# Two transformer blocks on one core: the halves of the values around the first pair, gate columns stationary, weighted sums one pair later, another order of the output units, x ahead of the weights

## The reference

```python
def first_block(x, ...):
    x = x + 0.5 * swiglu(rmsnorm(x, ff1_norm), w_gate, w_up, w_down)       # 2816 hidden columns
    h = rmsnorm(x, mix_norm)
    a_in, q, k, v, g_logits = split(h @ w_in)
    y_a = gmlp_spatial_gating(gelu(a_in), ...)
    y_b = stick_breaking_attention(q, k, v)     # 16 heads of 64, "stick"
    g_a, g_b = split(sigmoid(g_logits + b_gate))
    x = x + (g_a * (y_a @ w_branch_a) + g_b * (y_b @ w_branch_b)) @ w_out
    x = x + 0.5 * swiglu(rmsnorm(x, ff2_norm), ...)
    return rmsnorm(x, final_norm)

def second_block(x, ...):
    # layer 0: "moba"; with one block of 256 keys a causal softmax with a distance penalty
    # layer 1: "fox"; k, v and the gate from rms_norm(h, kv_norm):
    #   c = cumsum(log_sigmoid(hn @ w_f + b_f)); logit[t, s] += c[t] - c[s]
    for layer in range(2):
        h = h + merge_heads(mix) @ w_o[layer]
        h = h + squared_relu_mlp(rms_norm(h, mlp_norm[layer]), w_up[layer], w_down[layer])   # 4096 hidden
    return rms_norm(h, final_norm)
```

## Time and profile before

| | |
|---|---|
| runs, median (lowest to highest) | 1277.91 us (1277.82 to 1281.05) |
| the profiled execution, its time | 1278.92 us |
| its span, first to last instruction | 1277.2 us |
| mean granted TensorE clock | 0.992 |
| busy: TensorE, its weight loads | 97%, 83% |
| busy: VectorE, ScalarE, GpSimd | 64%, 50%, 14% |
| DMA | 213.20 MB on SP's queue, 173 GB/s over the span |

### The profile page before, as it was taken

One profiled execution on the slowest core, in us unless ns is written; L12 is line 12 of the kernel. 1 busy time (PEld: TensorE's weight loads), 2 busy tenths in 40 slices (PEclk: granted clock), 3 DMA queues, 4 the chain that ended last, 5 costly groups with the idle time before them and its releaser, 6 DMA issues.

```text
span 1277.2 us, 17745 instructions
## 1 busy us (share of the span) xinstructions
PE 1237.6 (97%) x6854; PEld 1055.8 (83%) x6854; DVE 823.2 (64%) x1272; ACT 636.6 (50%) x1012; POOL 176.3 (14%) x231
## 2 busy tenths in 40 slices
PE   6999999999999999999999999999999899999997
PEld 5788887898878878888878878888888887888886
DVE  4666667454686666666675757866654676786754
ACT  5444446555644346444456656544435465653442
POOL 0222220122030003221202310000000650000000
PEclk9999999999999999999999999999998999999999
DMA  6666655434646454565653445766551555575550
GB/s 193 204 217 213 209 189 175 124 111 140 219 146 228 144 166 153 191 199 198 198 181 117 140 149 182 259 201 190 190 166 34 166 170 169 173 251 194 186 178 34
DMA packets 175389, 221.77 MB, mean 174 GB/s; under 512 B 9804, under 2 KB 104632, under 8 KB 175304
## 3 DMA queue, kind: packets, MB, share of 16 engines
q1 hardware_dynamic: 173112, 213.20, 52.3%
q0 software_dynamic: 1888, 6.38, 1.6%
...
q10 hardware_dynamic: 304, 1.05, 0.2%
HBM read 219.53 MB, written 1.06 MB: 173 GB/s over the span
## 4 chain that ended last, share of the span: by engine, by line
PE 76%; DVE 10%; DMA 5%; ACT 3%; POOL 3%; issue 1%; SPq 1%; ACTq 0%; DVEq 0%; POOLq 0%
PE bank L1301 48%; PE bank L1381 15%; PE bank L1388 8%; DVE w_lo L882 5%; DMA raw<-in_ff_w_up 4%; POOL work L521 3%; ACT w_hi L584 1%; DVE work L935 1%; PE bank L1512 1%; PE bank L1324 1%; DVE xt L917 1%; PE bank L1499 1%; SPq L282 1%; DVE work L949 1%; ACT xt L621 1%
## 5 line engine op out<-in xcount | busy, mean ns | idle before, releaser
L882 DVE TENSOR_TENSOR w_lo<-raw,w_hi 128x512 fp32r<-128x512 f32 (+1 forms) x496 | 511.3, 1050 | 245.7 <-ACT w_hi L584 244.0
L584 ACT ACTIVATE w_hi<-raw 128x512 fp32r<-128x512 f32 (+1 forms) x496 | 431.9, 897 | 288.4 <-DMA raw<-in_ff_w_up 94.5
L1381 PE MATMUL bank<-xt,w_hi 128*128 128x512 f32 x1216 | 321.1, 396 | 4.1 <-DVE work L935 2.3
L1381 PEld LDWEIGHTS bank<-xt,w_hi 128*128 128x128 f32 x1216 | 216.5, 190 | 43.0 <-DVE work L935 3.2
L1388 PEld LDWEIGHTS bank<-xt,w_lo 128*128 128x128 f32 x1216 | 170.8, 190 | 15.4
L1388 PE MATMUL bank<-xt,w_lo 128*128 128x256 f32 x1216 | 175.2, 282 | 0.0
L1301 PE MATMUL bank<-w_hi,xt 128*128 128x512 f32 x512 | 161.6, 397 | 1.9 <-DVE w_lo L882 1.1
L1301 PE MATMUL bank<-w_hi,yt_lo 128*128 128x512 f32 x336 | 132.7, 395 | 2.0 <-DVE yt_lo L1048 2.0
L1301 PE MATMUL bank<-w_lo,yt_hi 128*128 128x512 f32 x336 | 131.6, 392 | 0.0
L1301 PE MATMUL bank<-w_hi,yt_hi 128*128 128x512 f32 x336 | 131.4, 391 | 0.0
L1301 PEld LDWEIGHTS bank<-w_hi,xt 128*128 128x128 f32 x512 | 96.2, 191 | 24.7 <-issue 3.9
...
## 6 DMA issues: line engine op xcount, KB each, us to landing
...
```

The lines of the kernel that those rows point to most:

```text
L584: act.activation(w_hi[:, c % RING, 0:w], raw[:, c % RAW, 0:w], ACT.Copy).then_inc(s["hi_ready"], 1)
L882: dve.tensor_tensor(w_lo[:, c % RING, 0:w], raw[:, c % RAW, 0:w], w_hi[:, c % RING, 0:w].bitcast(F32), ALU.subtract).then_inc(s["lo_ready" ...
L1381: ins = pe.matmul(up_banks(m)[q][:], w_h[:, k % 2, q * P:(q + 1) * P], flat(xt[:, k, :, :]), start=k == 0, stop=False, skip_group_check=True)
```

## The change

- **Units.** In the attention stages q and k of a pair come as one unit of 512 KB each, so a stage has 24 units instead of 40. `project(c, n, half)` takes half of one.
- **Opening.** Values half 0, then q and k of pair 0 (into banks 2 and 3), then values half 1 with the scores of pair 0 behind its first unit. `row_of_roots` on ScalarE comes earlier.
- **Cycle.** `weighted(pr - 1)` stands behind `middle(pr)` and ahead of the scores; `y_part` is a pair later on ScalarE and VectorE, and `second_part` waits for the weighted sums of the pair before.
- **Fox's gate.** The 16 columns of `wf` are stationary, and all 256 tokens move: 24 matmuls, rows of 16 partitions. The log of the gate is made in that shape, in parts of `c_all`, and turned back by two transposes (`gate_turns`).
- **Ends.** Behind moba and fox the units of `w_o` come in `OUT_ORDER`, of the two column halves in turn; behind stick `weighted(7)` follows the fourth unit of `a_in`.
- **Start.** x is the first DMA of SP's and of ScalarE's queue, `turn_ff1` has four banks, ScalarE's table is loaded first, TensorE makes 10 and 5 transposes of the identity, and the first chunk of ff1 waits for `hi` alone where it can.
- **Tail.** The last two units of mlp1 are taken token half by token half; of the output the first 512 columns are finished and sent by ScalarE, the last 512 by VectorE and SP.

```diff
+WARM = 10
...
+OUT_ORDER = ((0, 0), (0, 1), (0, 2), (1, 0), (0, 3), (1, 1), (1, 2), (1, 3))
...
+            return bank[4 + 2 * half:6 + 2 * half] if phase == "turn_ff1" else t_bank
...
+                def pair(u, pr):
...
+                        room(u + n, 0)
+                        send(u + n, 0, slot(u + n, 8, 1024), w[:, :, ds(pr * P, P)])
+                def values(first, e):
+                    for j in range(4):
+                        u = first + j
+                        room(u, 0)
+                        send(u, 0, slot(u, 2, 1024), v_w[:, 2 * j:2 * j + 2, e * 512:(e + 1) * 512])
+                values(b, 0)
+                pair(b + 4, 0)
+                values(b + 6, 1)
+                for pr in range(1, PAIRS):
+                    pair(b + RING + 2 * pr, pr)
...
+            def out_units(phase, w):
+                for n, (e, j) in enumerate(OUT_ORDER):
+                    c = at(phase, "units") + n
+                    room(c, 0)
+                    send(c, 0, slot(c, 2, 1024), w[:, 2 * j:2 * j + 2, e * 512:(e + 1) * 512])
+            sp.dma_start(x[:, 0, :], x_in[0, 0:P, :]).then_inc(s["x_in"], 16)
...
+            act.dma_start(x[:, 1, :], x_in[0, P:2 * P, :]).then_inc(s["x_in"], 16)
...
+            act.preload_act_table_set("sqrt_and_others")
...
+                    if pr:
+                        act.wait_ge(s["y_ready"], at(phase, "y_ready") + pr)
...
-                    hi(c + 4)
+                    if soft and pr:
+                        y_part(pr - 1)
                     first_part(pr + 1, 1 - e)
-                    hi(c + 5)
-                    y_part(pr)
-                    hi(c + 6)
-                    hi(c + 7)
+                    hi(c + 2)
+                    if not soft and pr:
+                        y_part(pr - 1)
+                    hi(c + 3)
...
                 hi(b + 6)
...
                 if phase == "fox":
+                    row_of_roots()
+                    values(0)
+                    hi(b + 7)
...
+                    first_part(0, 0)
+                else:
+                    hi(b + 7)
+                    if phase == "moba":
+                        act.wait_ge(s["rprod_done"], 1)
+                    values(0)
+                    hi(b + 8)
+                    row_of_roots()
+                    hi(b + 9)
+                    first_part(0, 0)
+                    hi(b + 10)
+                    hi(b + 11)
                 values(1)
-                act.wait_ge(s["rbc_ready"], at(phase, "rbc_ready") + 1)
...
+                else:
+                    second_part(PAIRS - 2, 0)
+                    first_part(PAIRS - 1, 1)
+                    hi(b + 26)
+                    y_part(PAIRS - 3)
+                    y_part(PAIRS - 2)
...
+                    dve.wait_ge(s["rbc_done"], at(phase, "rbc_done") + 1)
...
+                    dve.tensor_tensor(fz, bank[5][0:HEADS, 0:S], rbc[0:HEADS, :], ALU.mult).then_inc(s["fz_done"], 1)
...
+                    dve.tensor_scalar(fm, fz, bf[:], 0.0, ALU.add, ALU.min).then_inc(s["fm_done"], 1)
...
+                    dve.tensor_tensor(logft, fm, fe, ALU.subtract).then_inc(s["logft_done"], 1)
+                    lo(b + 7)
+                    q_evac(b + 4, 0, bank[2])
+                    dve.wait_ge(s["lt_ready"], 1)
...
+            add_half("mlp1", None, 0, at("mlp1", "units") + RING * N_MLP - 3)
...
+                dve.wait_ge(s["half_done"], 2 * tok + 1)
+                dve.tensor_tensor(x[:, tok, first], x[:, tok, first], row_gain[:, first], ALU.mult)\
...
+                v = x[:, tok, second]
+                dve.scalar_tensor_tensor(v, bank[2 + tok][:], rstd_sq[:, tok:tok + 1], v, ALU.mult, ALU.add)\
...
+                dve.tensor_tensor(side[:, tok, second], v, row_gain[:, second], ALU.mult)\
...
+                dve.tensor_scalar(side[:, tok, second], side[:, tok, second], rstd_f[:, tok:tok + 1], None, ALU.mult)\
...
+                        if m == 0 and j < 3:
+                            pe.wait_ge(s["hi_ready"], c + j + 1)
...
+                            if m == 0:
+                                ready(c + j)
...
+                    ready(c + 2)
+                    unit(2, (0,))
+                    ready(c + 3)
+                    unit(3, (0,)).then_inc(s["tail_ready"], 1)
+                    unit(2, (1,)).then_inc(s["used"], 1)
+                    unit(3, (1,)).then_inc(s["used"], 1)
...
+                def project(c, n, half, banks=(q_bank, k_bank)):
+                    if half == 0:
...
+                    w = slot(c + n, 8, 1024)
+                    for k in range(4 * half, 4 * half + 4):
...
+                        pe.wait_ge(s["w_done"], hp + 2 * pr)
...
+                    if pr:
+                        pe.wait_ge(s["y_lo"], at(phase, "y_lo") + pr)
...
+                def cycle(c, pr, e):
                     middle(pr, e)
+                    if pr:
+                        weighted(pr - 1, 1 - e)
                     scores(pr + 1, 1 - e)
...
-                    project(c, i, 3)
+                    project_pair(c)
...
+                def gate_rows():
                     pe.wait_ge(s["wf_lo_done"], 1)
+                    for k in range(KT):
+                        ins = three(bank[5][0:HEADS, 0:S], [v[:, k, :] for v in (wf_hi, wf_lo)],
+                                    part(xkv, k, slice(0, S)), k == 0, k == KT - 1)
+                    ins.then_inc(s["f_ready"], 1)
...
+                        ins = pe.transpose(bank[5][:, o:o + HEADS], logft[:, tok * P:(tok + 1) * P],
...
+                def first_pair(n):
+                    for half in range(2):
+                        project(b + 4, n, half, (bank[2], bank[3]))
+                def first_scores():
+                    if kind == "fox":
+                        pe.wait_ge(s["cn_done"], 1)
+                    scores(0, 0)
+                if kind == "fox":
+                    token_rows(phase)
+                    gate_rows()
+                    first_pair(0)
+                    gate_turns()
+                    first_pair(1)
+                    gate_sums()
+                else:
+                    first_pair(0)
+                    first_pair(1)
+                    token_rows(phase)
+                rows_times(b + 6, 0, bank[6:8], xkv, hooks={1: first_scores})
...
+                project_pair(b + 10)
...
+                if kind == "stick":
+                    fill(0)
+                    weighted(PAIRS - 2, 0)
+                    fill(1)
+                    fill(2)
+                    middle(PAIRS - 1, 1)
+                    fill(3)
+                    weighted(PAIRS - 1, 1)
...
+            def out_unit(phase, n):
+                e, j = OUT_ORDER[n]
+                c = at(phase, "units") + n
+                ready(c)
+                pe.wait_ge(s["y_lo"], at(phase, "y_lo") - PAIRS + 2 * j + 2)
+                w = slot(c, 2, 1024)
+                for k in (2 * j, 2 * j + 1):
+                    for tok in range(TOK):
+                        ins = three(bank[4 * e + tok][:], part(YT, k, tok_cols(tok)), [v[:, k % 2, :] for v in w],
+                                    k == 0, k == KT - 1)
+                ins.then_inc(s["used"], 1)
...
+                pe.transpose(bank[3][:, 0:P], ident[:], ident[:])
```

406 lines of the change are left out of this document (223 added, 183 removed).

## The result

The changed kernel takes 1266.12 us, the median of 4 runs (1264.77 to 1267.93), against 1278.43 for the kernel before, the median of 4 runs beside it. The ratio is 0.9898, with a 95% interval of 0.9883 to 0.9913: 13 us less, between 11 and 15. The forecast was 1257.9, with most of its chances between 1250 and 1265. The direction was right, and of the 20 us forecast some 13 came.

What follows compares the result with a forecast made beforehand. TensorE was 97% busy, leaving only stage starts and ends, the tail and its clock after pauses to gain. The terms summed to -20.0 us from the median of 1277.91, giving 1257.9, forecast range 1254 to 1262.

Steps and rivals of the forecast that it cites:

- The start: Kernel start up to the matmul behind `wst`: earlier x, table loads and transposes save 4.8 us, bounds -2.5 and -6.5.
- x complete 2.4 us earlier: Kernel start: x's halves first on two queues come 2.4 us earlier, net 1.2 after gain_rows and five warm-up transposes.
- the four banks: Kernel start: x's second half no longer held for the first's low parts, a 3.2 us wait of which 1.0 counts.
- Stick cycles: Six stick cycles: wide copies ahead of the sums make the mask late, +1.6 us, bounds -0.6 and +4.
- Stick's end: End of stick: mask wait covered, -0.8, but a new pause behind `weighted(7)`, +2.7; together +1.9 us.
- Its +2.7: Stick's end: TensorE has nothing to do behind `weighted(7)` while y_part, hi and lo follow, 2.7 us.
- Openings of stick and moba: Both openings: a unit of values covers the scores' wait for `kt`, -0.6 us each.
- Fox's opening: Fox's opening: wider gate matmuls, full clock and no wait for `kt` save 9.0 us, bounds -10 and -3.
- the +0.6 for `kt`: Fox's opening: late mask tables delay `kt` of pair 1 by 0 to 1.2 us, taken as +0.6.
- Ends of moba and fox: Stage ends: output units 2 and 3 cover the waits, -3.5 us; fox's slow clock goes, -1.7.
- Tail: Behind the last matmul: token half 0 finished early and a smaller store save 2.1 us.
- rival 3: New waits bite in fox's opening, x's bandwidth or stick's end, the last costing clock too: 1262 to 1268 us, chance 0.20.

Runs made afterwards that it cites:

- table: Changed kernel with ScalarE's table loaded where it was, ahead of the first x and again ahead of ff1's squares; 1269.86 us.
- x_act: Changed kernel with both halves of x on ScalarE's queue behind gain_rows, as before, and SP sending weights from the start; 1269.96 us.
- nowarm: Changed kernel without the fifteen warm-up transposes of the identity; 1261.99 us.
- cyc: Changed kernel with VectorE making the sums and qt ahead of the low part of unit c+2 in stick's cycles; 1262.17 us.
- stick_y28: stick_y plus unit 28, first of a_in's second half, copied ahead of stick's last y_part on ScalarE and VectorE; 1262.29 us.
- stick_y: Changed kernel with y_part of pair 5 ahead of unit 26 at stick's end, on ScalarE and VectorE; 1262.55 us.
- thin: Changed kernel plus fox's 48 old thin gate matmuls, result unused, ahead of the 24 new ones; 1278.26 us.
- xadd_kt: Changed kernel with VectorE's addition to x two low parts earlier in w_o0 and w_o1, and fox's pair 1 qt, kt ahead of unit 12's low part; 1259.14 us.
- out_linear: Changed kernel with the units of w_o0 and w_o1 in the old order, one column half after the other; 1268.93 us.
- tail_units: Changed kernel with both token halves of mlp1's unit 2 done before unit 3, which goes half by half; 1268.47 us.

## Why the prediction was wrong

- **The start**, -4.8 forecast, -4.3 measured. The size was about right and its shares were not, so that part is luck. The table loads gave their 2.6 (`table`). "x complete 2.4 us earlier", net 1.2, gave nothing at `wst` as a whole (`x_act`), and the transposes of the identity, partly priced within that step, cost 0.9 (`nowarm`). What is left, 1.7 where 1.0 was forecast for the four banks, is theirs and that of the matmuls that wait for `hi` alone, by subtraction; neither was tried by itself. The Trainium skill, "DMA: Bandwidth & Descriptors", section "Issuing engines are not separate DMA queues", has a second issuing engine save only the time of issuing. The same 25.1 in `x_act` agrees with that in the number, but no run here changes the queue alone.
- **Stick cycles**, +1.6 forecast, 1.8 measured. The mechanism was right: the step (the wide low part ahead of the sums) is shown by `cyc`, which takes it away and 1.1 us more.
- **Stick's end**, +1.9 forecast, 6.2 measured (7.0 with the moved `weighted`): here the prediction failed. The step was "The wait of 0.8 for the mask gets a whole unit as cover ... But `weighted(7)` now stands behind the fourth unit". Its +2.7 was right (-2.8 in `stick_y28`). What it put at nothing is the pair ahead: with `y_part` one pair late, `weighted(6)` has to wait for `yt_lo` of pair 5, and behind unit 26 on two engines that is 2.4 us, and in this execution 1.7 us of clock (`stick_y`: -3.2 for the stretch). The diff has the new wait in `weighted` in plain sight; the prediction followed the last pair and not the last but one.
- **Openings of stick and moba**, -0.6 each, measured -0.6 each.
- **Fox's opening**, -9.0 forecast, -10.0 to the first `middle`. The prediction's own terms add up to -9.35 and not to -9.0; without the +0.6 for `kt`, which falls behind the first `middle`, they give -9.95, which is what came. The rows' own 2.8 us and the clock are as argued, and `thin` shows both. The late tables were put at +0.6 for `kt` of pair 1, between 0 and 1.2 us. What was measured is 1.1 (8.9 against 7.7 in `xadd_kt`), near the upper end, by the way that the prediction told: the table, 9.7 us after the send and not 7.8, then ScalarE's `values(1)` and the low part of unit 12.
- **Ends of moba and fox.** The waits for `yt_lo` and for the weights went as forecast, and so did the slow clock in fox. `out_linear` gives back 1.0 of it in each stage. Left out was the far side of the same edit: ScalarE's and VectorE's `w_o` got one unit more behind the turn, and the addition to x came late, 1.1 more in each MLP than in the kernel before (`xadd_kt` takes 1.6 away in each).
- **Tail**, -2.1 forecast, -1.7 measured; half of it is the order by token halves (`tail_units`, 0.9).

Sum: of the 8 us between the forecast and the profile, 4.5 are stick's cycles and end, 2.2 the addition to x, 1.3 ff2's chance, 0.5 `kt`, 0.9 start and tail. Against them stand 1.4 us of gains beyond the forecast, in fox's opening and in the cycles and ends of moba and fox (their cycles gained 0.2 to 0.3 each instead of 0.1). The measured time lies in the range of rival 3, new waits that bite, but by luck: fox's opening returned nothing, and at stick's end the clock fell in this execution behind the wait for `yt_lo`, which no rival named, and not behind the 2.7 us pause.
